# HGRN decode states as the moving operand in groups of 32 columns, sums of squares ahead of the last gate tile, and column groups for two sums of the SSD layers

## The reference, cut to what matters

```python
# HGRN2, 8 heads of 128: state s is (128 keys x 128 values) for each head and sequence
q, fr, iv, gate = split(u @ w_in, 4)
q = silu(q); forget = lb + (1 - lb) * sigmoid(fr); k = 1 - forget; v = iv
# decode, for each sequence b and head h:   s = forget * s + k v^T ;  o = q @ s
# prompt, in chunks of 32 tokens: o = tril(qe ke^T) v + qe @ s_prev
o = rmsnorm(o, norm_g) * silu(gate)          # over the 128 values of a head
out = o @ w_out

# SSD
z, xbc, dt_raw = split(u @ w_in); xbc = silu(conv4(xbc)); dt = softplus(dt_raw + dt_bias)
y, h = ssd_scan(xs, dt, a, bm, cm, h0)
y = rmsnorm((y + xs * d_skip) * silu(z), norm_g)   # over all 2048 channels
out = y @ w_out
```

## Time and profile before

| what | value |
|---|---|
| median of three runs | 2213.59 us |
| profiled execution, its own time | 2212.78 us |
| span from first to last instruction | 2210.9 us |
| mean granted TensorE clock | 0.951 |
| PE matmul busy | 2070.1 us (94%) |
| DVE, ACT, POOL busy | 782.2, 590.0, 116.5 us |
| HBM traffic | 600.31 MB read, 35.56 MB written |

### The profile page before, as it was taken

How to read it: one execution, slowest core, us unless ns; L and a number is a source line. 1 busy time by engine, 2 the same in 40 slices (tenths; PEclk the granted TensorE clock), 3 DMA queues, 4 the chain that set the end, 5 groups by cost and what they waited for, 6 DMA issues and landing times. The chain is left out here.

```text
span 2210.9 us, 29922 instructions
## 1 busy us (share of the span) xinstructions
PE 2070.1 (94%) x11027; PEld 1343.6 (61%) x11027; DVE 782.2 (35%) x1852; ACT 590.0 (27%) x1352; POOL 116.5 (5%) x96
## 2 busy tenths in 40 slices
PE   6989989998999679989998999989998999989998
PEld 5877754444776356654445879654444877864444
DVE  3599132222012246332222251232223489422221
ACT  3486121112111115321112322121112477221111
POOL 0232000001000000000000000000000133100000
PEclk9999999999989759999999997799999999999999
DMA  7889489997746636389997455289997789569996
GB/s 259 252 277 267 133 340 422 421 421 263 242 137 236 201 108 245 109 337 421 421 421 282 139 151 163 95 345 421 421 421 281 208 284 282 160 248 420 422 421 280
DMA packets 249717, 628.99 MB, mean 284 GB/s; under 512 B 14120, under 2 KB 177112, under 8 KB 199816
## 3 DMA queue, kind: packets, MB, share of 16 engines
q1 hardware_dynamic: 230856, 607.51, 73.8%
q10 hardware_dynamic: 16384, 11.57, 1.7%
q0 software_dynamic: 2368, 8.48, 1.2%
HBM read 600.31 MB, written 35.56 MB: 288 GB/s over the span
## 5 line engine op out<-in xcount | busy, mean ns | idle before, releaser
L1518 PE MATMUL bank<-ring,e_xg 128*64 128x512 f32 x1536 | 336.6, 594 | 0.0
L657 PE MATMUL bank<-uT,ring 128*128 128x264 f32 x1280 | 293.6, 388 | 0.0
L657 PEld LDWEIGHTS bank<-uT,ring 128*128 128x128 f32 x1280 | 240.5, 190 | 46.0 <-issue 6.6
L1518 PEld LDWEIGHTS bank<-ring,e_xg 128*64 128x64 f32 x1536 | 107.5, 137 | 211.1 <-issue 202.4
L1546 PE MATMUL bank<-e_late,e_hT 128*64 128x512 f32 x1024 | 226.8, 595 | 2.7 <-ACT e_hT L1662 2.7
L1418 DVE TENSOR_TENSOR xT<-xT,bank 128x264 f32<-128x264 f32 x256 | 109.9, 429 | 225.3 <-PE bank L1569 221.9
L1658 ACT ACT_TABLE_LOAD x32 | 41.1, 1283 | 460.5 <-PE bank L1518 460.5
L1410 DVE TENSOR_TENSOR e_hg<-e_sg,bank 128x512 f32<-128x512 f32 x32 | 22.0, 688 | 390.0 <-PE bank L1518 390.0
L1546 PEld LDWEIGHTS bank<-e_late,e_hT 128*64 128x64 f32 x1024 | 70.7, 137 | 134.8 <-issue 127.9
L2824 PE MATMUL bank<-uT,ring 128*128 128x264 f32 x512 | 123.4, 402 | 6.1 <-PEq L213 6.1
L1494 PE MATMUL bank<-e_to_row,e_u_nat 128*128 128x128 f32 x1024 | 127.6, 280 | 0.0
(11 more groups left out here) (483 smaller groups left out, 2330.1 us busy)
## 6 DMA issues: line engine op xcount, KB each, us to landing
ring<-in_moe_w SPq DMA_DIRECT2D x192, 1024.0 KB, 10.5
e_late<-in_moe_w SPq DMA_DIRECT2D x192, 1024.0 KB, 12.3
ring<-in_m_w_in SPq DMA_DIRECT2D x40, 1024.0 KB, 8.6
s_hbuf<-in_ssm SPq DMA_DIRECT2D x32, 512.0 KB, 6.1
out_ssm_s<-s_hbuf SPq DMA_DIRECT2D x32, 512.0 KB, 3.5
ring<-in_m_w_out SPq DMA_DIRECT2D x16, 1024.0 KB, 6.8
ring<-in_h_w_in SPq DMA_DIRECT2D x16, 1024.0 KB, 8.3
...
```

What stands on the lines that cost most here:

```text
L657: mm = nc.tensor.matmul(bank[p % 3][0:m, 0:T], lhs, uT[:, k], start=(k == 0), stop=(k == KT - 1))
L1518: mm = nc.tensor.matmul(bank[b][CAP * j:CAP * j + CAP, :], xg[:, EK // 2 * h + k, CAP * j:CAP * j + CAP], rows_of(key)[:, k], start=(h + k ...
```

## The change

Four things are changed.

1. HGRN decode reads. `read_states(half)` does four sequences at once: for each head and each r of 0 to 3, the query column of sequence 4 half + r, repeated 32 times, is the stationary operand (32 columns, output partitions 32r to 32r + 31) and the 128x128 state moves. ACT copies the two banks to `od` (the space of `ke`), and `turn_decode(half)` picks one row of each group of 32 and turns it with eight matmuls of 128x4, into bank 4.
2. HGRN order. The first four states are read ahead of rows(0); rows(1), rows(2) and rows(3) stand together behind tile 28; the other four states are read behind them; tiles 29, 30 and 31 stand between the reads, the turn, the sum over heads and the spread. ACT squares the rows of each pair of heads when it has copied them, scales states 4 and 5 ahead of taking tile 28, and takes tile 31 after the root. DVE gates seven heads before tile 31. SP asks for states 4 to 7 together; a MoE weight transfer that stood between them goes behind the state stores.
3. HGRN sums. The eight heads are summed in four groups of 32 output partitions, two heads in each, and spread from there; root and reciprocal run on 128 partitions.
4. SSD. The dt projection is made in four groups of 32 partitions (two input chunks in each), and DVE adds the groups to `dtr` with three adds; PE's tile 3 waits for those. `sums(g)` uses four groups of 32 columns; ACT copies the bank, and one more matmul with ones (`spread_sums`, after output tile 1) adds the groups, before the root.

Cut to its core:

```diff
--- before.py
+++ after.py
...
+    c["one_of"] = (np.arange(33)[None, :] == 1) * np.ones((128, 1))
...
                     if p == 3:
-                        pe.wait_ge(*zed_taken.at(1))
+                        pe.wait_ge(*dt_added.at(3))
...
                     for k in range(KT):
                         if p == 0:
-                            lhs, m = w_dt[:, j, k], MH
+                            r = 32 * (k % 4)
+                            mm = nc.tensor.matmul(bank[0][r:r + 32, 0:T], w_dt[:, j, k], uT[:, k], start=(k < 4), stop=(k >= 4))
                         else:
                             s, _, c = place(p)
-                            lhs, m = W.view(s, KT, 256)[:, k, c:c + 128], 128
-                        mm = nc.tensor.matmul(bank[p % 3][0:m, 0:T], lhs, uT[:, k], start=(k == 0), stop=(k == KT - 1))
+                            mm = nc.tensor.matmul(bank[p % 3][:, 0:T], W.view(s, KT, 256)[:, k, c:c + 128], uT[:, k], start=(k == 0), stop=(k == KT - 1))
                     mm.then_inc(*tile_filled.one())
...
                 def sums(g):
 
                     pe.wait_ge(*square_done.at(g + 1))
-                    for k in range(4 * g, 4 * g + 4):
-                        mm = nc.tensor.matmul(bank[7][:, 0:T], ones, zT[:, k], start=(k == 0), stop=(k == CI - 1))
+                    for k in range(4):
+                        mm = nc.tensor.matmul(bank[7][32 * k:32 * k + 32, 0:T], ones[:, 0:32], zT[:, 4 * g + k], start=(g == 0), stop=(g == NG - 1))
                     if g == NG - 1:
                         mm.then_inc(*sums_made.one())
+
+                def spread_sums():
+
+                    pe.wait_ge(*sums_kept.at(1))
+                    nc.tensor.matmul(bank[7][:, 0:T], ones, part[0], start=True, stop=True).then_inc(*sums_spread.one())
...
                     out(t)
+                    if t == 1:
+                        spread_sums()
...
                 act.wait_ge(*sums_made.at(1))
-                nc.scalar.activation(rs, bank[7][:, 0:T], ACT.Sqrt, bias=eps[:, 0:1], scale=1.0 / DI).then_inc(*root_done.one())
+                nc.scalar.copy(part[0], bank[7][:, 0:T]).then_inc(*sums_kept.one())
+                act.wait_ge(*sums_spread.at(1))
+                nc.scalar.activation(rs, bank[7][:, 0:T], ACT.Sqrt, bias=eps[:, 0:1], scale=1.0 / (32 * DI)).then_inc(*root_done.one())
...
                 dve.wait_ge(*zed_taken.at(1))
+                for r in range(1, 4):
+                    nc.vector.tensor_tensor(dtr, dtr, bank[0][32 * r:32 * r + 32, 0:T], ALU.add).then_inc(*dt_added.one())
+                    dve.wait_ge(*dt_added.at(r))
                 link(nc.vector.scalar_tensor_tensor(out=s1, in0=dtr, scalar=-1.0, in1=dtr, op0=ALU.mult, op1=ALU.max))
...
+    ROWS = (3, 4, 7, 3)
...
+        od = ke[:].rearrange("p (o h) t -> p o (h t)", o=2)
...
                 for b in range(HBS, NB):
                     load_state(b)
-                    if b == HBS + 1:
-                        W.send(sp, first + SLOTS + 15)
...
                     if j == 0:
                         pe.wait_ge(*chunk_kept.at(2 * (NHC - 1)))
                         pe.wait_ge(*att_kept.at(HH))
+                    if j == 3:
+                        pe.wait_ge(*o_kept.at(1))
+                    b = bank[ROWS[j]]
                     for h in (2 * j, 2 * j + 1):
...
-                            nc.tensor.matmul(bank[3 + j][:, o + 128 * t:o + 128 * t + 128], vn[:, t, 128 * h:128 * h + 128], att[:, h, t],
+                            nc.tensor.matmul(b[:, o + 128 * t:o + 128 * t + 128], vn[:, t, 128 * h:128 * h + 128], att[:, h, t],
...
-                def read_state(b):
-
-                    pe.wait_ge(*s_done.at(b + 1))
-                    if b == 0:
-                        pe.wait_ge(*att_kept.at(HH))
+                def read_states(half):
+
+                    pe.wait_ge(*s_done.at(4 * half + 4))
+                    if half:
+                        pe.wait_ge(*od_copied.at(2))
                     for h in range(HH):
-                        mm = nc.tensor.matmul(bank[7][:, NB * h + b:NB * h + b + 1], sbuf[:, b % HBS, h], qT[:, h, LP + b:LP + b + 1], start=True, stop=True)
-                    mm.then_inc(*s_read.one())
+                        for r in range(4):
+                            b = 4 * half + r
+                            mm = nc.tensor.matmul(bank[5 + h // 4][32 * r:32 * r + 32, 128 * (h % 4):128 * (h % 4) + 128],
+                                                  qT[:, h, LP + b:LP + b + 1].to_broadcast([128, 32]), sbuf[:, b % HBS, h], start=True, stop=True)
+                            if h == HH - 1:
+                                mm.then_inc(*s_read.one())
+
+                def turn_decode(half):
+
+                    pe.wait_ge(*od_copied.at(2 * half + 2))
+                    if half == 0:
+                        pe.wait_ge(*o_kept.at(2))
+                    for h in range(HH):
+                        a = NB * h + 4 * half
+                        mm = nc.tensor.matmul(bank[4][:, a:a + 4], od[:, half, 128 * h:128 * h + 128],
+                                              ident[:].rearrange("p (j r) -> p r j", j=4)[:, 0], start=True, stop=True)
+                    mm.then_inc(*od_turned.one())
+
+                def sum_heads():
+
+                    pe.wait_ge(*o_squared.at(5))
+                    for h in range(HH):
+                        k = h // 4
+                        mm = nc.tensor.matmul(bank[7][32 * (h % 4):32 * (h % 4) + 32, 0:T], cst("one_of")[:, 1 - k:33 - k], sq[:, h],
+                                              start=(k == 0), stop=(k == 1))
+                    mm.then_inc(*o_sums.one())
+
+                def spread_roots():
+
+                    pe.wait_ge(*o_root.at(2))
+                    for h in range(HH):
+                        if h >= 4:
+                            pe.wait_ge(*o_normed.at(h - 3))
+                        r = 32 * (h % 4)
+                        nc.tensor.matmul(bank[3 + h % 4][:, 0:T], ident[r:r + 32, r + h // 4:r + h // 4 + 1].to_broadcast([32, 128]), rs[r:r + 32],
+                                         start=True, stop=True).then_inc(*root_spread.one())
...
-                for b in range(HBS):
-                    read_state(b)
-                for j in range(4):
+                read_states(0)
+                rows(0)
+                tile(28)
+                for j in range(1, 4):
                     rows(j)
-                    tile(28 + j)
-                for b in range(HBS, NB):
-                    read_state(b)
-                for h in range(HH):
-                    pe.wait_ge(*o_squared.at(h + 1))
-                    if h == 0:
-                        pe.wait_ge(*od_kept.at(1))
-                    mm = nc.tensor.matmul(bank[7][0:HH, 0:T], cst("pick")[:, 7 - h:15 - h], sq[:, h], start=(h == 0), stop=(h == HH - 1))
-                mm.then_inc(*o_sums.one())
-                pe.wait_ge(*o_root.at(2))
-                for h in range(HH):
-                    if h >= 4:
-                        pe.wait_ge(*o_normed.at(h - 3))
-                    nc.tensor.matmul(bank[3 + h % 4][:, 0:T], ident[0:HH, h:h + 1].to_broadcast([HH, 128]), rs[0:HH], start=True,
-                                     stop=True).then_inc(*root_spread.one())
+                read_states(1)
+                tile(29)
+                turn_decode(0)
+                turn_decode(1)
+                tile(30)
+                sum_heads()
+                tile(31)
+                spread_roots()
...
                 def keep_rows(j):
 
                     act.wait_ge(*o_made.at(j + 1))
-                    nc.scalar.copy(oT[:, 2 * j:2 * j + 2, 0:LP], bank[3 + j][:].rearrange("p (h t) -> p h t", h=2)).then_inc(*o_kept.one())
+                    heads = slice(2 * j, 2 * j + 2)
+                    nc.scalar.copy(oT[:, heads, 0:LP], bank[ROWS[j]][:].rearrange("p (h t) -> p h t", h=2)).then_inc(*o_kept.one())
+                    act.wait_ge(*o_kept.at(j + 1))
+                    nc.scalar.activation(sq[:, heads, 0:LP], oT[:, heads, 0:LP], ACT.Square).then_inc(*o_squared.one())
+
+                def copy_decode(half):
+
+                    act.wait_ge(*s_read.at(4 * half + 4))
+                    for k in range(2):
+                        nc.scalar.copy(od[:, half, 512 * k:512 * k + 512], bank[5 + k][:]).then_inc(*od_copied.one())
...
-                for j in range(4):
-                    take(28 + j)
-                    keep_rows(j)
-                    scale(HBS + j)
-                act.wait_ge(*s_read.at(NB))
-                nc.scalar.copy(oT[:, :, LP:T], bank[7][:, 0:64].rearrange("p (h b) -> p h b", h=HH)).then_inc(*od_kept.one())
+                copy_decode(0)
+                keep_rows(0)
+                scale(4)
+                scale(5)
+                take(28)
+                keep_rows(1)
+                scale(6)
+                scale(7)
+                keep_rows(2)
+                keep_rows(3)
```

(26 more changed lines are left out.)

4 lines of the change are left out of this document (3 added, 1 removed).

## The result

The changed kernel takes 2197.07 us (median of four runs, 2195.22 to 2198.01), the kernel before in the same session 2213.19; ratio 0.9928, 95% interval 0.9913 to 0.9943. That is 16.1 us less; 2193.0 was forecast, with a range of 2187 to 2204. The profiled execution of the changed kernel has a span of 2194.5 against 2210.9.

The account below looks back on a forecast made before the run. PE, busy 94% and slow-clocked at the HGRN layer's end, was taken as the bound, the states as a second chain. HGRN -14.4, SSD +1.3, -2.6 and -4.4 sum to -20.1 from 2212.8: about 2193, range 2187 to 2204.

Parts of the forecast that it names:

- SSD part: Both SSD layers: dt projection +1.3 us in the first, -2.6 in the second; sums -2.2 in each.
- The groups of the projection: First SSD layer, dt projection: the three DVE adds delay conv(1) and PE's tile 4, +1.3 us.
- The fall of the clock behind tile 4: First SSD layer: PE's wait before tile 4 may lose the clock again, 1.7 us, even odds.
- The column groups overlap at the full clock: Grouped records: four run at once, 0.027 us a record at clock 1.00, 0.053 at 0.50.
- this rival: Reads, sums, dt projection: column groups do not overlap at full clock, +16 us, 2209; chance 0.07.
- The states set the end: HGRN: arrival of state 4 and v broadcasts set the last update, 1368.3 instead of 1382.1; PE waits 19 us.
- What stands behind the wait: HGRN, last update to output projection: reads, turn, tiles 29 to 31, sum; effective start 1388.9, 16.9 us earlier.
- One more fall of the clock: HGRN, turn or spread: one more stretch at clock 0.50, 2.5 us set against the gain.
- the case "the clock": Rival: two more half-clock stretches, in turn and spread, and one in the first SSD layer, +5 us, 2198; chance 0.15.
- The rival of the broadcasts: HGRN, before the second reads: v broadcasts and states land late, +5.8 us, 2199; chance 0.12.
- The rival of the MoE layer: MoE layer's start waits for weights instead of the layer, HGRN gain lost, 2207; chance 0.05.
- The slower rival: HGRN: with three tiles behind the reads, v of sequence 7 landing after 1386 loses the whole gain; chance 0.03.

Follow-up runs that it names:

- e10: Changed kernel with the old dt projection (one column group, no adds) in both SSD layers, sums still in groups: 2201.5 us, ratio 0.9951.
- e3: Changed kernel with the old dt projection, without the adds, in the first SSD layer only: 2195.7 us, ratio 0.9933.
- e7: Changed kernel with three v buffers, tiles 29 to 31 and first turn ahead of the second reads, dt groups only in second SSD layer: 2179.7 us.
- e1: HGRN part of the change alone, both SSD layers as in the kernel before: 2201.9 us, ratio 0.9954.
- e8: Changed kernel with the old one-column decode reads, without copy and turn, in the new order: 2197.5 us, ratio 0.9930.
- e4: Changed kernel plus a one-column Silu behind the root, so ACT's table loads under tile 31: 2196.7 us, ratio 0.9932.
- e9: Changed kernel with the HGRN tiles back in their old places, column groups and joint request for states 4 to 7 kept: 2188.1 us, ratio 0.9892.
- e2: SSD part of the change alone, HGRN layer as in the kernel before: 2210.4 us, ratio 0.9994.

## Why the prediction was right, and where it was off

The time came out in the range, by the mechanism that was forecast: a new wait for the states, and a shorter tail behind it. The prediction's own steps follow; all ends are put on the time of the changed kernel, whose HGRN layer starts 1.9 us earlier than before's (1200.4 and 1202.3).

- **SSD part: right in the second layer, partly by luck in the first.** -0.9 and -4.8 were forecast for the two layers, the two traces give -0.8 and -4.9. In the second layer both terms hold: projection -2.6 (e10: -2.7), sums -2.2 (e10: -2.2). In the first, the sums give 2.1 to 3.3 (e3, e7 and e10 against before). The groups of the projection were put at +1.3 and cost about 2.8 on the mean of the traces. The seven traces of the changed layer average 257.1, the two of the old one (257.2, and 256.6 in e1) 256.9, so the change gained nothing there that can be seen, and the -0.8 of the two traces is scatter. The fall of the clock behind tile 4, given even odds, is in four of the seven. The new wait before tile 4 was put at 3 us and is 2.28 (2.1 to 3.2 in the other traces); the wait before output tile 0 was put at 2.4 and is 2.43. One reason was incomplete: in the second layer I held DVE's chain to be 3.0 us earlier, counted from the projection; it is 1.4 (5.7 us to L1091, where it was 7.12 to L1077), because DVE waits for the convolution state first. PE's tiles gained what was forecast all the same.
- **The column groups overlap at the full clock: right.** The first reads take 1.95 us for 64 records, 0.027 each after 0.2 to fill and drain; a sum takes 0.66 against 1.94, the projection 1.99 against 6.54. The Trainium skill, "TensorE: Matmul & The Clock Gate", section "Measured speedup vs the span model", has 2.38 for three groups. By the pace from one record to the next, four run at once here with no loss, at 1.00 too; a whole stage, with its filling and draining, was 2.9 times (the sum) to 3.3 times (the projection) shorter. The prediction's terms held 0.2 to 0.4 us for that already, so the 2 us more of the estimate by that page, 2195, did not come. The price of this rival was wrong in one term: by its own bound of 0.21 a record the second reads would cost 10 us more, not 5.7.
- **The states set the end: right.** The last update was put at 1368.3 on before's time, 1366.4 here, and ended at 1365.1. State 4 came 14.4 us after its request (14.9 used). The broadcast for sequence 6 took 9.8 us from its request at 1348.3 (10.6 used), that for 7 landed 4.9 later (4.2 used). PE's wait was put at 19 and is 17.7; that it swallows the first reads' gain was right, and e8 shows it: with the reads back at 11.4 us (and no copy and no turns) the layer is 0.3 us longer.
- **What stands behind the wait: too small.** This is the term that was mis-sized. -14.4 was forecast for HGRN, -10.2 measured (-9.4 at the start of the output projection). From the last update to the effective start of the output projection 20.6 us were forecast and 2.5 for the clock, 23.1 in all. It took 28.6: 26.2 to the start, and half of the 4.7 us that the projection still ran at 0.50. The 5.5 us between them are these:
  1. "Root and reciprocal lie under tile 31" held, but not the load of ACT's table for that tile, 1.3 us on the path; e4 takes it away.
  2. One more fall of the clock was set against the gain. There were two: the second, in the spread and the output projection, costs 2.4, where 2.5 were set, the first, from 1375.5 to 1379.0, 1.7 on top. That is the case "the clock" of the rivals without its part in the first SSD layer.
  3. The first output tile was to start 0.8 us after the first of the eight products and started 2.9 after it, because PE takes the spreads of heads 4 to 7 first, which wait for the products: 2.1.
  4. A record of the turn takes 0.11 us at 1.00 (28 in 3.00 us), not 0.09: 0.6.
  5. The clock was back when tile 29 began, which gives back the 0.7 set for that; the rest, 0.5, is mostly the three tiles, 3.7 us each and not 3.5.

  The last update was 1.3 early, and 4.2 us remain.
- **The rival of the broadcasts** did not happen; they were early. **The rival of the MoE layer** did not either: from the turn of the logits to the first matmul with the MoE layer's weights it took 18.7 us before and 18.6 in the changed kernel. **The slower rival** named the right place: three tiles that used to cover the updates now stand behind them. I priced it only as the point where the whole gain is gone. I did not ask what the groups would give without that move; e9 shows 9 us more.

The 0.09 was half of 0.18, the mean of the old reads, read as a time at 0.50. But each series of them began at the full clock, so 0.18 mixes the two levels:

```profile
1327.90:1330.40 2.50, 2.50 (x25) 2.50 (x23) 0.22 (x1) 0.39 (x1) 0.00 (x0) 1.00 0.64 220
1330.40:1339.20 8.80, 8.80 (x43) 8.80 (x43) 0.00 (x0) 0.00 (x0) 0.00 (x0) 0.50 0.91 203
```

With x us a record at 1.00 and 2x at 0.50, the 11.4 us of the first series make x = 0.11, as in the turns.

What is open: the medians of e1 and e2 leave 3.6 us of the whole unexplained, e10's 3 us. Stretches outside the changed layers differ from kernel to kernel although their code is the same, most of all the one from the logits of the first MoE layer to those of the second, with the attention layer in it. It took 660.2 us before, 659.5 in the changed kernel, 661.9 and 661.6 in e1 and e2, 660.7 in e10, and 656.0 to 662.0 over all traces, with 99 to 116 us of it at 0.50. In these single traces that is as much as the parts lack to the whole; whether it holds for the medians, and what moves the half-clock periods, was not settled.
